# A transformer layer in float32 on one core: first transfers reordered and split, last norm computed by ScalarE and taken from PSUM

## The reference

```
x = x + 1/2 * SwiGLU_1(RMSNorm(x))
h = RMSNorm(x); p = h @ W_in
x = x + (sigmoid(g_A) * (y_A @ W_A) + sigmoid(g_B) * (y_B @ W_B)) @ W_out
x = x + 1/2 * SwiGLU_2(RMSNorm(x))
out = RMSNorm_final(x)        # y = x * rsqrt(mean(x*x) + 1e-6) * g
```

## Time and profile before

| | |
|---|---|
| median of 3 runs | 1257.85 us (1257.71 to 1260.59) |
| the profiled execution | 1259.62 us |
| its span, first to last instruction | 1257.8 us |
| mean granted TensorE clock | 0.969 |
| TensorE busy | 1206.3 us, 96% |
| VectorE, ScalarE, GpSimd busy | 677.5, 444.4, 121.4 us |
| HBM read and written | 105.02 MB, 4.19 MB |

### The profile page before, as it was taken

One profiled execution on the slowest core, in us unless ns is written; L12 is line 12 of the kernel. 1 busy time (PEld: TensorE's weight loads), 2 busy tenths in 40 slices (PEclk: granted clock), 3 DMA queues, 4 the chain that ended last, 5 costly groups with the idle time before them and its releaser, 6 DMA issues.

```text
span 1257.8 us, 15631 instructions
## 1 busy us (share of the span) xinstructions
PE 1206.3 (96%) x5776; PEld 987.4 (78%) x5776; DVE 677.5 (54%) x823; ACT 444.4 (35%) x617; POOL 121.4 (10%) x93
## 2 busy tenths in 40 slices
PE   6999999999999999999897999999999999999995
PEld 5788888888887777777686878888888888888883
DVE  4755555533335744444969775765555555552213
ACT  5322333322223345557544442544233322222220
POOL 3000000000010200000543420002000000000011
PEclk9999999999999999999878789999999999999997
DMA  5333222332224221211200002243222223333201
GB/s 172 117 100 100 100 93 90 105 128 100 85 73 162 84 67 51 67 60 42 72 30 18 33 17 84 84 168 101 100 87 97 88 96 100 106 126 104 92 23 67
DMA packets 28841, 109.79 MB, mean 87 GB/s; under 512 B 3456, under 2 KB 3584, under 8 KB 28416
## 3 DMA queue, kind: packets, MB, share of 16 engines
q1 hardware_dynamic: 26784, 101.72, 24.1%
q10 hardware_dynamic: 2016, 7.50, 1.6%
HBM read 105.02 MB, written 4.19 MB: 87 GB/s over the span
## 4 chain that ended last, share of the span: by engine, by line
PE 91%; DVE 5%; issue 1%; ACT 1%; ACTq 0%; DMA 0%; DVEq 0%; SPq 0%
PE ps L981 27%; PE ps L982 27%; PE ps L983 27%; PE ps L1192 2%; PE ps L1195 2%; PE ps L1060 1%; PE ps L1069 1%; PE ps L1085 1%; DVE state L915 1%; PE ps L1176 1%; DVE xT L640 1%; DVE w_lo L640 0%; DVE b_cum L640 0%; PE ps L1010 0%; PE ps L1120 0%
## 5 line engine op out<-in xcount | busy, mean ns | idle before, releaser
L981 PE MATMUL ps<-h_hi,w_hi 128*128 128x512 f32 x1040 | 416.7, 401 | 13.8 <-DVE w_lo L640 9.8
L982 PE MATMUL ps<-h_lo,w_hi 128*128 128x512 f32 x1040 | 408.2, 392 | 0.0
L983 PE MATMUL ps<-h_hi,w_lo 128*128 128x512 f32 x1040 | 407.8, 392 | 0.0
L640 DVE TENSOR_TENSOR w_lo<-raw,w_hi 128x1024 fp32r<-128x1024 f32 (+1 forms) x178 | 234.0, 1315 | 154.3 <-ACT w_hi L361 153.6
L981 PEld LDWEIGHTS ps<-h_hi,w_hi 128*128 128x128 f32 x1040 | 197.3, 190 | 69.9 <-issue 14.0
L361 ACT ACTIVATE w_hi<-raw 128x1024 fp32r<-128x1024 f32 (+1 forms) x178 | 196.9, 1108 | 121.0 <-PE ps L983 118.5
L982 PEld LDWEIGHTS ps<-h_lo,w_hi 128*128 128x128 f32 x1040 | 197.7, 190 | 42.0 <-issue 1.9
L983 PEld LDWEIGHTS ps<-h_hi,w_lo 128*128 128x128 f32 x1040 | 197.3, 190 | 42.3
L981 PE MATMUL ps<-g_hi,w_hi 128*128 128x512 f32 x352 | 136.9, 389 | 0.0
L982 PE MATMUL ps<-g_lo,w_hi 128*128 128x512 f32 x352 | 136.9, 389 | 0.0
L983 PE MATMUL ps<-g_hi,w_lo 128*128 128x512 f32 x352 | 136.9, 389 | 0.0
(11 more groups left out here) (217 smaller groups left out, 1203.0 us busy)
## 6 DMA issues: line engine op xcount, KB each, us to landing
raw<-up_dram SPq DMA_DIRECT2D x88, 512.0 KB, 3.2
raw<-down_dram SPq DMA_DIRECT2D x32, 704.0 KB, 3.9
raw<-proj_dram SPq DMA_DIRECT2D x26, 512.0 KB, 3.3
raw<-gates_dram SPq DMA_DIRECT2D x16, 512.0 KB, 3.3
raw<-branch_dram SPq DMA_DIRECT2D x8, 512.0 KB, 3.3
raw<-wout_dram SPq DMA_DIRECT2D x8, 512.0 KB, 3.3
xT<-xT_dram ACTq DMA_DIRECT2D x8, 256.0 KB, 7.1
x_spill_dram<-xT ACTq DMA_DIRECT2D x1, 2048.0 KB, 7.4
```

Source lines behind the costliest of these rows:

```text
L640: return V.tensor_tensor(out, a, b, op)
L981: T.matmul(ps[:, bank, :], w_hi[:, slot, cols], moving_hi(j), start=start and j == 0, stop=False)
L982: T.matmul(ps[:, bank, :], w_hi[:, slot, cols], moving_lo(j), start=False, stop=False)
L983: ins = T.matmul(ps[:, bank, :], w_lo[:, slot, cols], moving_hi(j), start=False, stop=stop and j == tiles - 1)
```

## The change

At the start SP issues the transfers of x tiles 0, 2, 4 to 7, of the first weight unit in two halves, of the second unit, and of the two constants; ScalarE issues only `gain` and x tiles 1 and 3. The split of the first unit is done in halves, the first half behind x tile 0, the second behind tile 2; the second unit is split behind tile 6. TensorE waits for the first half at block 0 and for the second at block 4. SP's loop over `up1` starts one step later.

At the end the matmuls over `sq_sum` are put ahead of the wait for the last square. The factor is computed by `Ln` and `Exp(-0.5 *)` on ScalarE with one Newton step on VectorE; the table set for it is loaded behind the up loop of the second feed-forward. VectorE multiplies its tiles, now 0 to 5, by the factor straight from PSUM bank 6. A second spread matmul writes bank 7, from which ScalarE copies `rs` for GpSimd, which has tiles 6 and 7. The order of the stores is another.

```diff
-        POOL_OUT = (5, 6, 7)
+        tail_v, tail_y, tail_spread = sem("tail_v"), sem("tail_y"), sem("tail_spread")
+        POOL_OUT = (6, 7)
+        first_raw, first_hi, first_lo = sem("first_raw"), sem("first_hi"), sem("first_lo")
+        HALF = UW // 2
...
         @block.sync
         def _(sp):
+            sp.dma_start(xT[:, 0, :], xT_in[:, 0, :]).then_inc(x_loaded[0], 16)
+            sp.dma_start(raw[:, 0, 0:HALF], up1[0, :, 0:HALF]).then_inc(first_raw, 16)
+            sp.dma_start(xT[:, 2, :], xT_in[:, 2, :]).then_inc(x_loaded[2], 16)
+            sp.dma_start(raw[:, 0, HALF:UW], up1[0, :, HALF:UW]).then_inc(raw_loaded[0], 16)
+            for n in (4, 5, 6, 7):
+                sp.dma_start(xT[:, n, :], xT_in[:, n, :]).then_inc(x_loaded[n], 16)
+            sp.dma_start(raw[:, 1, 0:UW], up1[1, :, :]).then_inc(raw_loaded[1], 16)
+            sp.dma_start(small[:], small_const).then_inc(small_loaded, 16)
+            sp.dma_start(lbl[:], lb_logits).then_inc(lb_loaded, 16)
...
-                with sp.Fori(0, count // 2) as it:
+                with sp.Fori(1 if name == "up1" else 0, count // 2) as it:
...
-            for n in (0, 1, 5, 2, 3, 6, 4, 7):
+            for n in (0, 1, 2, 6, 3, 4, 7, 5):
...
             nc.scalar.preload_act_table_set("sigmoid_and_others")
-            for n in range(KT):
+            for n in (1, 3):
                 act.dma_start(xT[:, n, :], xT_in[:, n, :]).then_inc(x_loaded[n], 16)
-            act.dma_start(small[:], small_const).then_inc(small_loaded, 16)
-            act.dma_start(lbl[:], lb_logits).then_inc(lb_loaded, 16)
...
                 up_body(FT // 2 - 1, True)
+                if k == 2:
+                    nc.scalar.preload_act_table_set("natural_log_exp_and_others")
...
-                if n in (0, 4):
-                    split_hi(n // 4)
+                if n == 0:
+                    act.wait_ge(first_raw, 16)
+                    A(w_hi[:, 0, 0:HALF], raw[:, 0, 0:HALF], ACT.Copy).then_inc(first_hi, 1)
+                if n == 2:
+                    act.wait_ge(raw_loaded[0], 16)
+                    A(w_hi[:, 0, HALF:UW], raw[:, 0, HALF:UW], ACT.Copy).then_inc(hi_done, 1)
+                if n == 6:
+                    split_hi(1)
...
+            act.wait_ge(tail_v, 1)
+            A(norm_y[:], norm_v[:], ACT.Ln).then_inc(act_seq, 1)
+            act.wait_ge(act_seq, 5 + PAIRS + 1)
+            A(norm_y[:], norm_y[:], ACT.Exp, scale=-0.5).then_inc(tail_y, 1)
+            act.wait_ge(tail_spread, 1)
+            A(rs[:], ps[:, TAIL_BANK, :], ACT.Copy).then_inc(rs_done, 1)
...
-                if n in (0, 4):
-                    split_lo(n // 4)
+                if n == 0:
+                    dve.wait_ge(first_hi, 1)
+                    tt(w_lo[:, 0, 0:HALF], raw[:, 0, 0:HALF], w_hi[:, 0, 0:HALF].bitcast(F32), ALU.subtract).then_inc(first_lo, 1)
+                if n == 2:
+                    dve.wait_ge(hi_done, 1)
+                    tt(w_lo[:, 0, HALF:UW], raw[:, 0, HALF:UW], w_hi[:, 0, HALF:UW].bitcast(F32), ALU.subtract).then_inc(lo_done, 1)
+                if n == 6:
+                    split_lo(1)
...
-            rms_factor(3)
-            rms_rows(3)
+            dve.wait_ge(mean_done, 4)
+            V.tensor_scalar(norm_v[:], ps[:, MEAN_BANK, 0:ST], 1.0 / D, EPS, ALU.mult, ALU.add).then_inc(tail_v, 1)
+            dve.wait_ge(tail_y, 1)
+            link(newton(norm_y[:], norm_v[:], norm_t[:]))
+            diagonal()
+            dve.wait_ge(spread_done, 4)
             for n in range(POOL_OUT[0]):
                 dve.wait_ge(scaled, n + 1)
-                tt(xT[:, n, :], xT[:, n, :], rs[:], ALU.mult).then_inc(out_dve, 1)
+                tt(xT[:, n, :], ps[:, MEAN_BANK, :], xT[:, n, :], ALU.mult).then_inc(out_dve, 1)
...
+            def first_unit_wait(j):
+                pe.wait_ge(h_done, j + 1)
+                if j == 0:
+                    pe.wait_ge(first_lo, 1)
+                if j == KT // 2:
+                    pe.wait_ge(lo_done, 1 + RAW_CREDIT)
...
+            def mean_of_the_last():
+
+                pe.wait_ge(sum_done, 8 * 3 + 7)
+                for j in range(ST):
+                    cols = slice(P * j, P * (j + 1))
+                    T.matmul(ps[:, MEAN_BANK, j:j + 1], sq_sum[:, cols], ones[:, 0:1], start=j == 0, stop=False)
+                pe.wait_ge(sq_done, 8 * 3 + 8)
+                for j in range(ST):
+                    cols = slice(P * j, P * (j + 1))
+                    ins = T.matmul(ps[:, MEAN_BANK, j:j + 1], sq[:, cols], ones[:, 0:1], start=False, stop=j == ST - 1)
+                ins.then_inc(mean_done, 1)
...
-            mean(3)
+            mean_of_the_last()
             spread(3)
+            T.matmul(ps[:, TAIL_BANK, :], ones, sq[:], start=True, stop=True).then_inc(tail_spread, 1)
```

More of the change, by code:

```diff
@@ L175, in build @@
         ps = ctx.enter_context(nc.psum_tensor("ps", [P, 8, S], F32))
-        UP_BANKS, RES_BANKS, MEAN_BANK, Y_BANKS = (0, 2), 4, 6, (6, 7)
+        UP_BANKS, RES_BANKS, MEAN_BANK, TAIL_BANK, Y_BANKS = (0, 2), 4, 6, 7, (6, 7)
         raw_loaded = [sem(f"raw_loaded{i}") for i in range(RAW_SLOTS)]
@@ L668, in rms_factor, with diagonal @@
                     link(newton(norm_y[:], norm_v[:], norm_t[:]))
+                diagonal()
+            def diagonal():
                 tt(sq[:].rearrange("p (a b) -> p a b", b=P), ident.unsqueeze(1).to_broadcast([P, ST, P]),
@@ L991, in h_wait @@
                 return lambda j: pe.wait_ge(h_done, 8 * m + j + 1)
+            def first_unit_wait(j):
[4 more added lines that the diff above has]
+                    pe.wait_ge(lo_done, 1 + RAW_CREDIT)
             def mean(m):
-                pe.wait_ge(sum_done, 8 * m + (8 if m < 3 else 7))
+                pe.wait_ge(sum_done, 8 * m + 8)
                 if m == 0:
                     pe.wait_ge(small_loaded, 16)
-                if m == 3:
-                    pe.wait_ge(sq_done, 8 * m + 8)
                 for j in range(ST):
                     cols = slice(P * j, P * (j + 1))
-                    ins = T.matmul(ps[:, MEAN_BANK, j:j + 1], sq_sum[:, cols], ones[:, 0:1], start=True, stop=m < 3)
-                    if m == 3:
-                        ins = T.matmul(ps[:, MEAN_BANK, j:j + 1], sq[:, cols], ones[:, 0:1], start=False, stop=True)
+                    ins = T.matmul(ps[:, MEAN_BANK, j:j + 1], sq_sum[:, cols], ones[:, 0:1], start=True, stop=True)
+                ins.then_inc(mean_done, 1)
[8 more added lines that the diff above has]
+                    ins = T.matmul(ps[:, MEAN_BANK, j:j + 1], sq[:, cols], ones[:, 0:1], start=False, stop=j == ST - 1)
                 ins.then_inc(mean_done, 1)
@@ L1018, in up_body @@
                             cst = base + 2 * q + w
-                            pe.wait_ge(lo_done, cst + 4 * it + 1 + RAW_CREDIT)
+                            head = first and q == 0 and w == 0
+                            if not (head and m == 0):
+                                pe.wait_ge(lo_done, cst + 4 * it + 1 + RAW_CREDIT)
                             pe.wait_ge(read, f0 + 2 * it + q + 1)
-                            wait = h_wait(m) if first and q == 0 and w == 0 else None
+                            wait = (first_unit_wait if m == 0 else h_wait(m)) if head else None
                             h_unit(UP_BANKS[w] + q, cst, wait).then_inc(unit_done, 1)
```

## The result

Five timed runs of each, and later six of the changed kernel beside eleven of the one before:

| | before | changed | ratio, 95% interval |
|---|---|---|---|
| first timing | 1260.27 us (1257.71 to 1261.02) | 1251.23 us (1249.05 to 1255.14) | 0.9945 [0.9925, 0.9964] |
| second timing | 1259.47 us (1255.68 to 1260.99) | 1254.0 us (1252.22 to 1255.25) | 0.9959 [0.9945, 0.9974] |
| profiled execution, span | 1259.62, 1257.8 | 1255.14, 1253.3 | |

What follows compares the result with a forecast made beforehand. TensorE, 91% busy, bounds the kernel, so only its start and end can gain: 1.5 + 4.0 = 5.5 us off 1257.85 gives 1252.35 us. Own range 1251.3 to 1253.4; 8 in 10, 1250.3 to 1254.4.

Steps and rivals of the forecast that it cites:

- Head, start: At the kernel's start, the half unit lands at about 5.0 us and TensorE starts at 6.4, 3.35 earlier.
- Head, who is late next: In the first unit, tile 7 waits behind unit 1's split; its first matmul comes at 14.8 against 16.44, gain 1.6.
- The half microsecond that I gave for unmixed queues: At the start, unit 1's transfer may land half a microsecond sooner, since only two x tiles mix with SP's queue.
- Cover of the squares: Before unit 3, earlier squares leave 2.2 us of cover against 1.6 needed, so the gain at the start passes on.
- The clock: In the first unit, the slow matmul pace may last until tile 7; 0.1 us deducted, leaving a gain of 1.5.
- Table load: On ScalarE behind the second feed-forward's up loop: 1.3 us, hidden by a 3.40 us wait for TensorE, costing nothing.
- Tail: From last residual to end of span: mean 0.96, factor 0.85, spread 0, products and stores 2.19; gain 4.0 us.
- The row with an operand in PSUM: VectorE's final products: 0.69 us each, unblocked by GpSimd, against 1.26 with two SBUF operands.
- the late piece: At the end, GpSimd's second tile, tile 7, is done at 1250.4 us and the last store goes out at 1250.85.
- Sum: Whole kernel: 1.5 us gained at the start plus 4.0 at the end, 5.5 us.
- The rival of no head: At the start, tile 7 as late as before or TensorE's clock falls; only the end gains, 1253.9 us, chance 0.15.
- The rival of half a tail: At the end, GpSimd blocked, slow ScalarE hand-overs or queued stores leave 2.0 to 2.5 of 4.0 us, chance 0.12.

Runs made afterwards that it cites:

- the second profile: The changed kernel, unaltered, profiled once more: span 1252.3 us; its timed runs had median 1254.0 us, ratio 0.9959 to the kernel before.
- the head alone: Changed kernel with the end of the kernel before, keeping only the new first transfers, half units and split order: 1257.56 us, ratio 0.999 to before.
- the tail alone: Changed kernel with the start of the kernel before, keeping only the new end: 1255.36 us, ratio 0.9962 [0.9947, 0.9976] to before.

## Why the prediction was right, by its steps

- **Head, start**: 6.4 predicted, 7.14 seen (6.81 in the second profile). The term that was too small is the first landing: ScalarE waited for `gain`, issued at 0.75, until 4.75, a transfer that had landed 1.7 us after its issue before, and the half unit came at 5.6 and not at 5.0. It had no effect on the end, as the constant 14.73 us behind the landing of unit 1 shows.
- **Head, who is late next**: right in kind and place, shown by moving unit 1 behind tile 7. Mis-sized: the landing of unit 1. I took 11.6 within 11.0 to 12.2; ScalarE took it up at 12.34, and between 11.71 and 13.24 over the eight profiles with this order of transfers. The half microsecond that I gave for unmixed queues was not there: 340 GB/s from 2 to 11 us before, 340 again in the changed kernel. And more bytes came first than the 3.17 MB that I counted: 3.57 MB had been moved by 12.29, so 0.4 MB belonged to transfers issued behind unit 1 (the constants and unit 2), worth 1.2 us at 340 GB/s. (By the sum's own numbers 3.17 MB are in at 11.3 and not 11.2, and the path from w_hi to the next h_lo before is 3.13 and not 3.15 us; both are too small to matter. In the changed kernel that path was 3.03.) Tile 7's first matmul was at 15.37 and not 14.8. The gain was 0.93 and not 1.5 in this profile, and 1.50 in the second, where ScalarE took unit 1 up at 11.77: the sum was right where its landing came nearly true.
- **Cover of the squares**: w_lo of unit 3 was ready at 24.88 + 2.31 = 27.19 against a start of unit 3 at 27.87. It held with 0.68 us to spare, where the prediction had 2.2 - 1.6 = 0.6. The squares began at 13.91 and not at 13.2, but they hang on the same landing as the gain, so the two errors cancel.
- **The clock**: TensorE stood 1.57 us before tile 7 (0.56 to 1.90 over the five profiles with this head) and went on at 0.23 us a matmul: the level stayed. In this profile the slow pace ended 3.1 us after the first matmul, at 10.3 instead of 13.3. In the second it lasted 4.8 us, to 11.6, and the stand was 0.56 us, shorter than the 1.5 to 2 predicted; the end did not suffer, because the stand absorbs the length of the slow pace. The prediction brought in the Trainium skill, "TensorE: Matmul & The Clock Gate", "HAM oscillation — how this bites in real kernels", against this half. The kernel of that section has DMA waits of about 3 to 5 us between its bursts of matmuls; no wait before tile 7 is that long here, so these profiles neither bear it out nor contradict it, and it was no argument against a stand of 2 us.
- **Table load**: nothing, with the cover that the row had shown.
- **Tail**: all four differences within 0.05 us. The row with an operand in PSUM was the right one of the two. The Trainium skill, "SBUF — State Buffer", "Who interferes with whom", says that a VectorE instruction with at most one SBUF input does not contend with GpSimd; 3.68 against 5.83 us for six products agrees. The spread ran at the lower level, as taken. Not right was the late piece: SP's queue was set back by GpSimd's first tile, some 0.1 us more than by its second.
- **Sum**: 5.5 against 5.1 and 5.5 outside the recurrent stage. The rival of no head is excluded by the profiles (0.93 and 1.5), though the timed runs of the head alone do not tell its 1.3 us from nothing. The rival of half a tail is excluded by the interval of the tail alone.
- What the prediction did not have: the spread of 5 us in the recurrent stage. The first median, 1251.23, is 1.1 us under the forecast, inside the range for 8 in 10 and just outside the forecast's own (1251.3 to 1253.4). That it landed so near is in part luck: in the same timing the kernel before had 1260.27 and not the 1257.85 that the forecast starts from.

## What to carry to other kernels

When a first product starts earlier, look for the operand that is now last in the queue, and for what stands ahead of it on the engines that convert it: here 2.6 us at the start were 0.9 to 1.5 at the end of the third unit, and one step in the order of the splits gave 1.3 more at an equal landing. When a landing varies from execution to execution, measure from it: the time behind it was the same to 0.04 us in five profiles whose ends differ by 0.9. Differences in a serial tail can be summed from rows to a tenth of a microsecond, one handover after another. To time a change of a few microseconds, take the stage whose clock level varies out of the spans before comparing.

## What the runs showed of the hardware

- The recurrent stage takes between 142 and 147 us from execution to execution, with granted clocks of 0.66 to 0.91 in the same window (620 to 640 us). From the start of the fifth unit (36.93 before, 36.00 changed) to the first scan it is 584.2 to 584.4 us in all ten profiles.
- A 21 KB transfer on ScalarE's queue, issued at 0.75 with a 256 KB one on SP's queue, landed after 4.0 us (3.6 to 4.0 in the eight profiles with this order); 0.3 us ahead of SP's first transfer it had landed after 1.7.
- Transfers issued behind a large one on the same queue moved bytes before it landed: 3.57 MB by 12.29 us, where those up to it were 3.17 MB.
- The matmuls of the first unit ran at half pace for 3.1 to 5.3 us, and for 3.1 and 4.8 us in two executions of the same kernel, while the profile's granted clock read 1.00.
- Waits of 0.56 to 1.90 us before tile 7 left the pace at 0.23 us a matmul.
- With both operands in SBUF and GpSimd at work, VectorE's 128x512 products came 1.67 us apart; with GpSimd idle, or one operand in PSUM, they took 0.6.
